# Layer 1's expert outputs are summed token-major onto x in PSUM, and the last norm reads these sums

## The reference, cut to what matters

```python
for l in range(DEPTH):                       # DEPTH = 2
    ...
    x = x + hierarchical_moe(rms_norm(x, ffn_norm[l]), ...)   # 32 experts, top 2
return rms_norm(x, final_norm)

def rms_norm(x, g):
    y = x * lax.rsqrt(jnp.mean(x * x, axis=-1, keepdims=True) + EPS)
    return y * g
```

## Time and profile before

| | us |
|---|---|
| median of 3 runs | 1674.19 |
| lowest, highest | 1673.24, 1674.54 |
| the profiled execution | 1668.83 |
| its span, first to last instruction | 1667.0 |
| mean granted TensorE clock in it | 0.909 |
| busy in the span: PE | 1324.9 (79%) |
| PEld, DVE, ACT | 1020.6, 587.1, 448.4 |
| mean DMA rate over the span | 320 GB/s |

### The profile page before, as it was taken

How to read it: one execution, slowest core, us unless ns; L and a number is a source line. 1 busy time by engine, 2 the same in 40 slices (tenths; PEclk the granted TensorE clock), 3 DMA queues, 4 the chain that set the end, 5 groups by cost and what they waited for, 6 DMA issues and landing times.

```text
span 1667.0 us, 30744 instructions
## 1 busy us (share of the span) xinstructions
PE 1324.9 (79%) x13385; PEld 1020.6 (61%) x13385; DVE 587.1 (35%) x916; ACT 448.4 (27%) x648; POOL 0.4 (0%) x5
## 2 busy tenths in 40 slices
PE   6999999998677675767677999998987655666665
PEld 5999999985354352535347999997944323433332
DVE  6658746544121201102016785565421100110102
ACT  6454444532120111011014445445310000101001
POOL 0000000000000000000000000000000000000000
PEclk8999999999889798988867999998999987987886
DMA  9843458349999999999997326672699999999993
GB/s 346 297 167 115 152 179 334 131 155 392 417 426 422 427 427 423 426 423 427 427 390 262 122 94 211 247 260 101 239 384 428 427 427 427 426 427 425 427 428 157
DMA packets 94021, 534.19 MB, mean 320 GB/s; under 512 B 10018, under 2 KB 14522, under 8 KB 67900
## 3 DMA queue, kind: packets, MB, share of 16 engines
q1 hardware_dynamic: 90900, 522.24, 78.0%
q10 hardware_dynamic: 2984, 9.91, 1.5%
HBM read 525.84 MB, written 6.29 MB: 319 GB/s over the span
## 4 chain that ended last, share of the span: by engine, by line
PE 51%; DMA 39%; DVE 6%; issue 2%; ACT 2%; SPq 0%; DVEq 0%; ACTq 0%
DMA ring<-in_w_expert_out 32%; PE banks L1541 28%; DMA ring<-in_w_expert_in 6%; PE banks L1568 6%; PE banks L1918 5%; PE banks L1874 4%; PE banks L1929 2%; PE banks L1891 1%; DVE stat L1402 1%; PE banks L1738 1%; DVE w_lo L954 1%; PE banks L1754 1%; PE banks L1676 0%; DVE arena L1397 0%; DVE xT L1097 0%
## 5 line engine op out<-in xcount | busy, mean ns | idle before, releaser
L1874 PE MATMUL banks<-ring,arena 128*32 128x256 f32 x3968 | 286.1, 439 | 152.0 <-DMA ring<-in_w_expert_in 145.4
L1874 PEld LDWEIGHTS banks<-ring,arena 128*32 128x32 f32 x3968 | 133.6, 123 | 284.9 <-DMA ring<-in_w_expert_in 179.2
L954 DVE TENSOR_TENSOR w_lo<-ring,w_hi 128x2048 fp32r<-128x2048 f32 (+1 forms) x105 | 215.1, 2049 | 133.9 <-ACTq L575 122.0
L1541 PE MATMUL banks<-h_hi,w_hi 128*128 128x256 f32 x784 | 223.3, 285 | 0.1
L1541 PE MATMUL banks<-h_hi,w_lo 128*128 128x256 f32 x784 | 221.8, 283 | 0.0
L1395 DVE TENSOR_TENSOR arena<-arena,banks 128x128 f32<-128x128 f32 x65 | 18.8, 289 | 564.7 <-ACT arena L909 564.7
L1918 PE MATMUL banks<-ring,arena 128*32 128x256 f32 x2016 | 147.7, 442 | 79.7 <-DMA ring<-in_w_expert_out 67.6
L909 ACT ACTIVATE arena<-banks 128x128 f32<-128x128 f32 x65 | 18.1, 278 | 697.1 <-PE banks L1874 697.1
L1541 PE MATMUL banks<-h_lo,w_hi 128*128 128x256 f32 x720 | 203.7, 283 | 0.0
L598 ACT CAST w_hi<-ring 128x2048 fp32r<-128x2048 f32 (+1 forms) x105 | 179.9, 1714 | 82.8 <-PE banks L1541 34.2
L1918 PEld LDWEIGHTS banks<-ring,arena 128*32 128x32 f32 x2016 | 72.5, 124 | 136.3 <-issue 49.7
(11 more groups left out here) (346 smaller groups left out, 2101.4 us busy)
## 6 DMA issues: line engine op xcount, KB each, us to landing
ring<-in_w_expert_in SPq DMA_DIRECT2D x124, 2048.0 KB, 23.7
ring<-in_w_expert_out SPq DMA_DIRECT2D x63, 2048.0 KB, 24.7
ring<-in_w_in SPq DMA_DIRECT2D x24, 2048.0 KB, 8.9
ring<-in_w_branch SPq DMA_DIRECT2D x12, 1024.0 KB, 5.0
ring<-in_w_out SPq DMA_DIRECT2D x4, 2048.0 KB, 7.9
ring<-in_w_xq SPq DMA_DIRECT2D x4, 2048.0 KB, 10.7
spare_unit<-in_w_expert_in SPq DMA_DIRECT2D x4, 2048.0 KB, 12.8
ring<-in_w_xo SPq DMA_DIRECT2D x4, 2048.0 KB, 7.9
```

The lines of the kernel that those rows point to most:

```text
L954: post(dve.tensor_tensor(piece_view(w_lo, *key), piece_view(ring, *key), high_view(*key).bitcast(F32), ALU.subtract), "w_split")
L1541: ins = pe.matmul(acc, stationary(a, k), moving(b, k), start=k == 0 and n == 0, stop=k == kc - 1 and n == 2)
L1874: ins = pe.matmul(G[32 * j:32 * j + 32, :], xTe[:, k, e * SL:(e + 1) * SL], w[:, k % 4, :, j * P:(j + 1) * P], start=k == 0, stop=k == KC - 1,
```

## The change

Layer 1's sums are made token-major. In L1929's matmuls `swt` is now the stationary operand and `ysb` the moving one (layer 0 keeps the old form), so a bank `j` holds, for both token blocks, features 256j to 256j+255 with the tokens on the partitions. `x` itself is added there too: in the first turn of layer 1, behind the turned weights of experts 4 to 7, TensorE multiplies pieces of `xT` with the identity onto the banks (`add_tokens`, 16 matmuls).

Behind the closing matmuls ScalarE squares the eight pieces 128x256 of the four banks, each with a running sum per token (`accum_out`), in the order of banks 0, 1, 2, 3; it waits for `y_full` ahead of bank 2. VectorE multiplies the banks by the norm's weight into `y_final`, in the order 2, 3, 0, 1, and waits for ScalarE's first four squares ahead of bank 0. Then come a sum of 4 values per token and block, one root and one reciprocal of 128x2. VectorE scales token block 0 in two halves and SyncE stores them; ScalarE scales block 1 in two halves and issues their stores itself. A root on a dummy value stands ahead of the waits.

The norm's weight is no longer in the prologue's rows (`ROW_FIN` is gone, 68 rows for 76). It is loaded behind `wo1` of layer 1 as one row copied to all partitions, into `lnt`. `add_x`, `pair_sums`, `norm`, the turning back and the copies are gone behind layer 1.

```diff
@@ SyncE
+                    if name == "wo1" and layer == L - 1:
+                        sp.wait_ge(S["vn_ready"], L)
+                        sp.dma_start(final_row, A["final_norm"].unsqueeze(0).broadcast_to([P, D])).then_inc(S["rows_loaded"], 16)
...
-            for i in range(4):
-                sp.wait_ge(S["out_ready"], i + 1)
-                sp.dma_start(out[0].rearrange("(t p) d -> t p d", p=P)[i % 2, :, (i // 2) * 512:(i // 2) * 512 + 512],
-                             arena[:, i * 512:(i + 1) * 512]).then_inc(S["stored"], 16)
+            for half in range(2):
+                sp.wait_ge(S["out_ready"], half + 1)
+                part = slice(half * 512, half * 512 + 512)
+                sp.dma_start(out[0].rearrange("(t p) d -> t p d", p=P)[0, :, part], y_final[:, 0, part]).then_inc(S["stored"], 16)
@@ ScalarE
-            x_norm(L, "norm0", False)
-            for i in range(4):
-                evac(L, "out", i, arena[:, i * 512:(i + 1) * 512], "out_ready", view=lambda a: a)
+            link(act.activation(small[:, 58:59], small[:, 95:96], ACT.Sqrt))
+            for j in range(4):
+                acc = two(job_wait(act, L - 1, "moe", j))
+                if j == 2:
+                    act.wait_ge(S["y_full"], 2 * L + 2)
+                for tb in range(TB):
+                    act.activation(hT[:, 2 * j + tb, :], acc[:, tb, :], ACT.Square,
+                                   accum_out=final_sq[:, 4 * tb + j:4 * tb + j + 1]).then_inc(S["ssq_ready"], 1)
+            act.wait_ge(S["ssq_biased"], L + 1)
+            link(act.activation(final_rms, final_sum, ACT.Sqrt, bias=small[:, 95:96], scale=1.0 / D))
+            act.sem_inc(S["rms_ready"], 1)
+            act.wait_ge(S["rstd_ready"], L + 1)
+            for half in range(2):
+                part = slice(half * 512, half * 512 + 512)
+                link(act.activation(y_final[:, 1, part], y_final[:, 1, part], ACT.Copy, scale=final_rstd[:, 1:2]))
+                act.dma_start(out[0].rearrange("(t p) d -> t p d", p=P)[1, :, part], y_final[:, 1, part]).then_inc(S["stored"], 16)
@@ VectorE
-                for i in range(4):
-                    add_x(layer, "moe", i)
-                    if i:
-                        pair_sums(i - 1)
-                pair_sums(3)
...
-            norm(ROW_FIN, 0, False)
+            for j in (2, 3, 0, 1):
+                acc = two(job_wait(dve, L - 1, "moe", j))
+                if j == 0:
+                    dve.wait_ge(S["ssq_ready"], 4 * L + 4)
+                part = slice(j * T, (j + 1) * T)
+                post(dve.tensor_tensor(y_final[:, :, part], acc, final_row[:, part].unsqueeze(1).broadcast_to([P, TB, T]), ALU.mult), "y_full")
+            dve.wait_ge(S["ssq_ready"], 4 * L + 8)
+            post(dve.tensor_reduce(final_sum, final_sq.rearrange("p (t j) -> p t j", t=TB), AX.X, ALU.add), "ssq_biased")
+            dve.wait_ge(S["rms_ready"], 2 * L + 1)
+            post(dve.reciprocal(final_rstd, final_rms), "rstd_ready")
+            for half in range(2):
+                part = slice(half * 512, half * 512 + 512)
+                post(dve.tensor_scalar(y_final[:, 0, part], y_final[:, 0, part], final_rstd[:, 0:1], None, ALU.mult), "out_ready")
@@ TensorE
-                                ins = pe.matmul(psum[:, j, c * T:(c + 1) * T], ysb[32 * j:32 * j + 32, c * P:(c + 1) * P],
-                                                swt[32 * j:32 * j + 32, :], start=False, stop=False,
+                                rows = slice(32 * j, 32 * j + 32)
+                                part = slice(c * P, (c + 1) * P)
+                                stationary, moving = (ysb[rows, part], swt[rows, :]) if layer + 1 < L else (swt[rows, part], ysb[rows, :])
+                                ins = pe.matmul(psum[:, j, c * T:(c + 1) * T], stationary, moving, start=False, stop=False,
...
+                    def add_tokens(e):
+
+                        if e >= 4:
+                            j = e - 4
+                            for tb in range(TB):
+                                for c in range(2):
+                                    at = tb * T + c * P
+                                    pe.matmul(psum[:, j, at:at + P], xT[:, 2 * j + c, tb * P:(tb + 1) * P], ident,
+                                              start=False, stop=False, skip_group_check=True)
```

More of the change, by code:

```diff
@@ L131, in plan_jobs @@
             ended.append(key)
+    ended += [(L - 1, "moe", i) for i in range(4)]
     for n, key in enumerate(ended):
@@ L301, in trunk @@
         sel = over("sel", arena_at, 10016, TB, EI, SL)
+        final_row = lnt.rearrange("p a b -> p (a b)")
+        y_final = region(0, TB, D)
+        final_sq, final_sum = small[:, 48:56], small[:, 56:58]
+        final_rms, final_rstd = small[:, 66:68], small[:, 68:70]
         ysb = stat[:, 0:T]
@@ L1491, in _ @@
                     split_to(layer + 1, "q", 0, ahead=0)
-                for i in range(4):
-                    add_x(layer, "moe", i)
-                    if i:
-                        pair_sums(i - 1)
-                pair_sums(3)
-                if layer + 1 < L:
-                    split_to(layer + 1, "q", 1, ahead=0)
-            norm(ROW_FIN, 0, False)
+                    for i in range(4):
+                        add_x(layer, "moe", i)
+                        if i:
+                            pair_sums(i - 1)
+                    pair_sums(3)
+                    split_to(layer + 1, "q", 1, ahead=0)
+            dve.wait_ge(S["rows_loaded"], 16 * 7)
+            for j in (2, 3, 0, 1):
[11 more added lines that the diff above has]
+                post(dve.tensor_scalar(y_final[:, 0, part], y_final[:, 0, part], final_rstd[:, 0:1], None, ALU.mult), "out_ready")
         @block.tensor
@@ L1988, in _ @@
                                    tile_position=(32 * j, 0)))
-            norm(L, "norm0")
-            for i in range(4):
-                pe.wait_ge(S["h_full"], 4 * (n_norm[0] + 1) - (2, 0)[i // 2])
-                acc = job_begin(pe, L, "out", i)
-                for c in range(4):
-                    ins = pe.transpose(acc[:, c * P:(c + 1) * P], hT[:, 4 * (i // 2) + c, (i % 2) * P:(i % 2 + 1) * P], ident)
-                done(ins)
 _INS = ['x', 'mem', 'positions', 'mix_norm', 'w_in', 'b_gate', 'attn_sinks', 'gmlp_ln_g', 'gmlp_ln_b',
```

14 lines of the change are left out of this document (6 added, 8 removed).

## The result

| | before | changed |
|---|---|---|
| median, us | 1671.06 (6 runs) | 1659.36 (6 runs) |
| lowest, highest | 1666.88, 1674.54 | 1656.35, 1664.14 |
| ratio of the times, 95% interval | | 0.9936 [0.9921, 0.9952] |
| the profiled execution, and its span | 1668.83, 1667.0 | 1658.68, 1656.8 |
| mean granted TensorE clock | 0.909 | 0.918 |

The kernel is faster, as forecast, and its profiled span is 10.2 us shorter (forecast 9.2). The median lies 5.6 us under the forecast of 1665.0 and 3.2 us under the low end of the range. The three runs shown ahead of the prediction were 1673.24 to 1674.54; the three that were added beside the changed kernel were 1666.88 to 1668.88. Against these three alone, whose median is 1668.02, the changed kernel is 8.7 us faster; against all six it is 11.7. The gain was forecast about right, then, and the level from which it was subtracted was not.

A forecast was written before the change was run, and what follows sets the result against it. Layer 1's weight stream, then an exposed 19.0 us tail, were taken to bound the kernel. The tail saves 9.2 us, other terms 0: span 1667.0 to 1657.8, profiled 1659.6, median 1665.0 us (-0.55%); range 1662.6 to 1668.4.

The forecast's parts named there:

- What bounds the kernel: Layer 1's expert weight stream on the DMA engines from about 1214 us, then the exposed final-norm tail of 19.0 us.
- (a) The new tail: Behind the closing matmuls: the norm's 19.0 us go, 9.8 come, so 9.2 us less, with bounds 8.0 to 10.1.
- the data term: End of the tail by the four stores' data: 1653.5 + 1.3 + 2.8 + 0.4 = 1658.0, against 1657.3 by issue alone.
- (b) The table load: Root's table loaded by a dummy root before the tail, over near 1645: cost nothing; uncovered 1.5 us.
- (c) The additions: x added by 16 matmuls in layer 1's first turn: cost 0; if all were exposed, 4.4 us.
- (d) The change of operands: Stationary and moving operand exchanged in layer 1's token sums, 8 matmuls as before: cost 0, either sign.
- (e) The norm's row: Norm's row loaded behind `wo1` on SyncE, ahead of `xq0`: cost 0; uncovered 1.2 us.
- (f) One load less: One small SyncE load less in the prologue: between 0 and 0.4 us gained, taken as 0.
- The late stream: Rival: additions delay layer 1's slot release and the norm's row meets `xq0`; 5.6 us come back, 1670.6; chance 0.10.
- TensorE as the bound: Rival: low clock in the 24 experts behind layer 1's first turn, 15.6 against DMA's 14.7 us each; 1687; chance 0.02.
- The squares at 0.87 us each: Rival: ScalarE's eight squares in the tail take 7.0 us instead of 4.0; time 1668.0; chance 0.06.
- the last of the sum: From the changed span 1657.8 to the median: 1.8 us over span gives 1659.6, 5.4 more gives 1665.0.

## Why the prediction was right and where it was wrong

**What bounds the kernel**: right. The stream of layer 1 is unchanged, and the file of work behind the last loads decides.

**(a) The new tail**: right in sum, by pieces that were off both ways. From the readers' start to the end of the span 9.8 us were forecast, measured were 1656.8 - 1647.2 = 9.6:

| piece | forecast | measured |
|---|---|---|
| squares, until the sum of squares starts | 4.0 | 3.5 (1647.21 to 1650.73) |
| sum, root, reciprocal | 0.9 | 0.9 |
| scaling, until the last store's issue | 1.95 | 1.9 (1651.62 to 1653.52) |
| last issue to the end | 2.95 | 3.3 |

The squares' pitch is 0.36, not the 0.50 taken and below the lower bound of 0.465: the step that counted the accumulator's read as part of the pitch was wrong. It had been taken from squares that wait for each other; without a wait the read runs on into the next square. The condition written behind VectorE's products ("costs nothing as long as a square takes over 0.4 us") was not met then: VectorE's four products, one every 0.85 us, take the squares' place as what ends last, so 8 x 0.36 = 2.9 us became 3.5. The end was 1652.30 + 1.3 + 2.8 + 0.4 = 1656.8 by the data term, which is what was measured, and the data's share over 1653 to 1656 adds up to the 2.8 us. I had forecast 1657.8 instead of that term's 1658.0. The Trainium skill (DMA: Bandwidth & Descriptors, "Issuing engines are not separate DMA queues") held here: the second issuer didn't bring a second rate, the four stores' 1.05 MB took 2.8 us of all engines. The Trainium skill's fixed 2.0 us plus bytes at 436 GB/s (the same page, "Anatomy of one DMA — SWDGE (gpsimd) path", a fit for transfers that GpSimd issues) gives an estimate of 1652.30 + 4.4 = 1656.7 for the end. That is close, but partly by luck: for one store of 262 KB the same form gives 2.6 us, and 2.0 were measured to the landing.

VectorE's scaling took 0.49 us for 512 columns, not 0.43, and the first store came 0.06 later for it. The row it was priced from (0.296 us at 256 columns) multiplies by a constant; the new one multiplies by a value per partition, and the kernel before has that form too: 0.354 us at 256 columns (L1198, eight times), 0.058 more. From there 256 columns more cost 0.13 us, where the two-source form pays 0.27 (0.42 at 256, 0.69 at 512). The Trainium skill (VectorE: DVE Perf Modes, "What auto-detection actually checks") lets this form take a doubled mode, and the halved price per column agrees with it.

The old tail was 19.34 to 19.50 us from the closing matmuls in three profiles, the new one 10.06 to 10.26 in five. The gain is 9.3 us; the forecast was 9.2. That the total came out within 0.1 us is partly luck, as the squares were 0.5 us too dear and the end 0.3 too cheap.

One reading of the old tail was wrong, though it cost the sum nothing, as the 19.0 us were taken as measured: "The clock matters little there: TensorE has only 20 short instructions". It had 24 records, busy for 8.4 us, and 4.1 us of them stand in the chain that ended last (2.09 us of sums from 1653.38, 1.98 us of turning back from 1661.91). From 1650.5 on its granted clock was 0.50, as in this stretch with the columns of the earlier trace rows:

```profile
1660.00:1662.00 2.00, 1.91 (x9) 1.51 (x10) 1.65 (x4) 0.73 (x2) 0.00 (x0) 0.50 0.00 0
```

The new tail has no TensorE in it, so part of what it saves is matmuls at half the clock.

**(b) The table load**: right. It ran at 1641.84 to 1643.12, and the dummy root was over 3.9 us before ScalarE was needed. ScalarE was through its branches 0.53 us behind its last copy, not the 1.4 taken from TensorE, which has a drain there too.

**(c) The additions**: cost 0, right, by another way. The forecast had 0.3 us per expert pushed out and given back at expert 6, where the wait should shrink from 2.17 by 0.6. The wait was 2.69, not smaller, and next to nothing was pushed out (1.27 against 1.23 us). I had laid lengths of records end to end, 0.44 + 1.1 = 1.5; but records on TensorE overlap: the additions begin 0.28 us behind the start of the turned weights, and the next product begins 0.99 behind theirs.

**(d) The change of operands**: right, cost 0 within 2 us (ratio 0.9997).

**(e) The norm's row**: right. SyncE's timeline shows the new issue, and `xq0` not later:

```profile
1054.80 0.58 SPq L476 DMA_DIRECT2D lnt<-in_final_norm  x1
1066.16 0.37 SPq L423 DMA_DIRECT2D ring<-in_w_xq  x1
```

It stands at 1066.16 instead of 1066.83, 0.67 earlier, as the load ahead of both (1048.73 against 1049.38).

**(f) One load less**: 0 fits; with the load put back neither the next issue (52.67 us) nor the median moved by more than the runs differ among themselves.

**The rivals.** The late stream (closing matmuls would be later than 1649) and TensorE as the bound (granted clock 0.81 there, as before) didn't come. The squares at 0.87 us each neither: it was 0.36.

**The failed step is the last of the sum**: "The median of the runs is 1674.19, 5.4 above the profiled one; the tail is the same work in all of them, so I subtract the same". That the tail is the same work holds. But the profiled execution was itself a draw from the same kernel, 5.4 us lower, and said that these three, within 1.3 us of each other, weren't the kernel's whole spread. What the runs showed in place of the 1674.19: later sets of the old kernel have medians of 1669.62 (23 runs), 1672.20 (11) and 1670.70 (11), and single runs from 1665.59 to 1676.03. Started from the profiled execution the same sum gave 1659.6, which the prediction also names; the median measured was 1659.36. That these two are so close is in part luck: the changed kernel's other medians are 1660.26 and 1661.52. The range then allowed "about 1 us for the chip and the build", where the old kernel's medians alone span 4.6 us between 1669.6 and 1674.2. The mean of all four executions at hand, 1672.7, would have given 1663.5, still too high; what was in reach was the range, which should have gone down to the profiled execution's own 1659.6 and the 1 us around it.

What stays open: why the first three runs lay together at 1673 to 1674.5. Of 57 later ones in the three sets six took 1673.24 or more. They may be from another chip or moment; runs without a trace don't tell in which of A to E their time lay. Open too is the first comparison's further 1 to 2 us beyond the tail (ratios 0.9936 and 0.9937, then 0.9945, where 9.3 us are 0.9944): all three intervals hold 0.9944, so nothing asks for another cause.

## What to carry to other kernels

Where a reduction ends a kernel, choose the layout in which its result is one value per partition: the norm needed no sum over partitions, no root of 256 columns and no turning back, and 19.5 us became 10.1. Price a tail piece by piece, but take the level from all executions at hand, the profiled one included, and give the range the spread between sets, not that within one. Where two engines read the same banks in opposite order, price both paths: one engine's whole work, and the other's first half followed by one's own second half. Here they were 0.13 us apart, so shortening one alone gave 0.13.

## What the runs showed of the hardware that I had not expected

- The accumulator's read (0.19 to 0.22 us) costs ScalarE nothing if the next square doesn't wait: 128x256 squares from PSUM follow each other at 0.36 us, less than the 0.38 of one.
- A drain, the read of a count from SBUF and the branch on it hold TensorE 1.26 to 1.37 us (ten profiles, three of them of the old tail). With the read ahead of the loop and the drain in the branch there is no gap at all, though the branch stays: in two profiles the closing matmuls began 0.96 us behind the start of the sums, beside the last of them.
- VectorE waiting for its own product and then signalling costs 0.2 to 0.25 us each: products of 0.69 us came every 0.85, and every 0.60 to 0.65 without it.
- A multiplication on VectorE by a value per partition costs 0.058 us more than one by a constant: 0.354 against 0.296 us at 128x256.
- Four stores of 262 KB, issued within 1.2 us from two engines, landed 2.4 to 2.9 us after issue; with the data of three of them cut, the whole one ended the span 2.4 us behind its issue, against 3.3.
- The last expert's second product took 1.93 us in eight profiles, at a granted clock of 1.00, and 2.5 to 3.6 us in four others, at 0.53 to 0.74. These dips came in some executions and not in others of one kernel, and cost 1.2 to 1.7 us here.
